# Splitting a layer's first weight tiles earlier: in the down gemm, and between the norm's column blocks

## The reference, cut to what matters

```python
for l in range(DEPTH):                       # DEPTH = 2
    mod = c_act @ w_ada[l] + b_ada[l]
    sh1, sc1, gt1, sh2, sc2, gt2 = split(mod, 6)
    h = rms_norm(x, norm_mix[l]) * (1.0 + sc1) + sh1
    proj = h @ w_in[l]                       # dn_qkv, dn_z, dn_a, dn_b, sw_q, sw_k, sw_v, gate_a, gate_b
    ...
    x = x + gt1 * (merged @ w_o[l])
    h = rms_norm(x, norm_ffn[l]) * (1.0 + sc2) + sh2
    up_act, up_lin = split(h @ w_up[l], 2)
    up_act = causal_dwconv(up_act, ffn_conv[l]) + ffn_conv_b[l]
    x = x + gt2 * ((silu(up_act) * up_lin) @ w_down[l])
# second block, one layer
h = rms_norm_2(x, norm_gain[0])
proj = h @ w_in[0]
...
```

## Time and profile before

| what | value |
|---|---|
| median of 3 runs | 2764.27 us (2758.3 to 2764.56) |
| the profiled execution | 2765.13 us, its span 2763.1 us |
| mean granted TensorE clock | 0.971 |
| PE busy | 2565.5 us, 93% |
| DVE busy | 1444.8 us, 52% |
| ACT busy | 1075.4 us, 39% |
| POOL busy | 918.6 us, 33% |

### The profile page before, as it was taken

The page is one execution under the profiler, slowest core; times in us unless marked ns, Lnnn a source line. Parts: engine busy times, 40 slices in busy tenths (PEclk is TensorE's granted clock), DMA queues, the critical chain, the costliest instruction groups (busy, mean ns, idle before and its releaser), DMA issues. The chain is left out here.

```text
span 2763.1 us, 32968 instructions
## 1 busy us (share of the span) xinstructions
PE 2565.5 (93%) x12929; PEld 2070.7 (75%) x12929; DVE 1444.8 (52%) x2609; ACT 1075.4 (39%) x1872; POOL 918.6 (33%) x402
## 2 busy tenths in 40 slices
PE   5989899899989999989988989999999997899998
PEld 3767768797867888757676878877788886786787
DVE  5289748654535541136993766454344206726323
ACT  3345464245332232243554523543333223236532
POOL 0532231112434444334222211134344443332343
PEclk8999999999999999999999989999999999999999
DMA  6211325643234432222132465422223324731232
GB/s 236 76 62 62 123 69 145 186 133 135 96 103 137 137 102 91 93 92 76 47 123 68 116 165 179 146 87 92 76 92 107 93 98 125 152 101 47 77 121 77
DMA packets 339836, 299.93 MB, mean 109 GB/s; under 512 B 56974, under 2 KB 319460, under 8 KB 338660
## 3 DMA queue, kind: packets, MB, share of 16 engines
q1 hardware_dynamic: 287716, 279.49, 32.5%
q10 hardware_dynamic: 51968, 18.35, 2.7%
HBM read 267.89 MB, written 29.93 MB: 108 GB/s over the span
## 5 line engine op out<-in xcount | busy, mean ns | idle before, releaser
L273 PE MATMUL ps<-hh,split 128*128 128x512 f32 x3808 | 1291.6, 407 | 39.4 <-POOL split L220 24.5
L220 POOL TENSOR_TENSOR split<-ring,split 128x1024 fp32r<-128x1024 f32 (+2 forms) x342 | 814.6, 2383 | 1428.4 <-ACT split L216 1428.4
L273 PEld LDWEIGHTS ps<-hh,split 128*128 128x128 f32 x3808 | 729.0, 191 | 212.5 <-POOL split L220 39.7
L273 PE MATMUL ps<-hl,split 128*128 128x512 f32 x1904 | 753.2, 396 | 0.0
L216 ACT ACTIVATE split<-ring 128x1024 fp32r<-128x1024 f32 (+2 forms) x342 | 347.6, 1018 | 893.1 <-PE ps L273 686.1
L273 PEld LDWEIGHTS ps<-hl,split 128*128 128x128 f32 x1904 | 365.4, 192 | 73.1 <-issue 8.4
L273 PE MATMUL ps<-split 128*128 128x512 f32 x1152 | 285.4, 405 | 9.0 <-DVE split L1095 7.1
L273 PEld LDWEIGHTS ps<-split 128*128 128x128 f32 x1152 | 218.6, 190 | 70.6 <-issue 14.7
L2169 PE MATMUL ps<-split 128*128 128x512 f32 x1056 | 240.2, 389 | 0.0
L2169 PEld LDWEIGHTS ps<-split 128*128 128x128 f32 x1056 | 198.1, 188 | 41.0
L560 POOL TENSOR_TENSOR split<-ring,split 128x1024 fp32r<-128x1024 f32 x32 | 76.1, 2378 | 338.2 <-ACT split L552 338.2
(11 more groups left out here) (408 smaller groups left out, 3178.2 us busy)
## 6 DMA issues: line engine op xcount, KB each, us to landing
ring<-in_w_in_dram SPq DMA_DIRECT2D x60, 1024.0 KB, 5.3
ring<-in_w_up_dram SPq DMA_DIRECT2D x44, 1024.0 KB, 5.1
ring<-in_w_ada_dram SPq DMA_DIRECT2D x64, 512.0 KB, 3.7
ring<-in_w_in_dram SPq DMA_DIRECT2D x34, 512.0 KB, 5.2
big<-in_w_ada_dram SPq DMA_DIRECT2D x16, 1024.0 KB, 8.5
ring<-in_w_down_dram SPq DMA_DIRECT2D x16, 896.0 KB, 4.6
ring<-in_w_swa_out_dram SPq DMA_DIRECT2D x8, 1024.0 KB, 5.0
ring<-in_w_dn_out_dram SPq DMA_DIRECT2D x8, 1024.0 KB, 5.0
```

Of the source, the lines that this page charges most:

```text
L220: on.tensor_tensor(halves(pt, nk)[1], slot(n, nk)[:, :, e * P:(e + 1) * P], halves(pt, nk)[0], ALU.subtract).then_inc(low_made, 1)
L273: ins = nc.tensor.matmul(ps[bank[gt]][0:m, :], w[:, k, :], r[:, k, :], start=(k == 0 and w is w_high and r is rhs[0]), stop=(k == nk - 1 a ...
```

## The change

Five edits. (1) TM's high and low parts get a home of their own (`tm_split`, in `wk` 4, 5, 10, 11) and are made before the layer's block: for layer 0 in the setup block, for layer 1 at the end of layer 0's down gemm. (2) In the layer's block ACT starts with the 16 columns, and puts SW's two high parts behind column blocks 3 and 5 of the norm. (3) The 16 columns' low part goes from POOL to DVE, and POOL starts SW's low parts when seven of the eight `hl` blocks are done. (4) The low parts of the activations follow one block behind instead of two, at all three norms. (5) `mix_sum` moves from `wk` 10 to `kd_flat` in layer 0, since `wk` 10 now holds TM's low part.

```diff
+            tm_split = [split[:, SPLIT_WK + a:SPLIT_WK + a + 2, :].rearrange("p a c -> p (a c)").rearrange(
+                "p (k c) -> p k c", k=KD) for a in (4, 10)]
+            tm_high, tm_low = sem("tm_high"), sem("tm_low")
...
+            def split_tm_high(act, l):
+                act.wait_ge(early[l][TM], 16)
+                nc.scalar.activation(tm_split[0], slot(TM)[:, :, 0:P], ACT.Copy).then_inc(tm_high, 1)
+            def split_tm_low(pool):
+                pool.wait_ge(tm_high, 1)
+                nc.gpsimd.tensor_tensor(tm_split[1], slot(TM)[:, :, 0:P], tm_split[0], ALU.subtract).then_inc(tm_low, 1)
...  (setup block)
+                        split_tm_high(act, 0)
                         mix_rs_of(act)
+                    @block.gpsimd
+                    def _(pool):
+                        split_tm_low(pool)
...  (a layer's first block, ACT)
-                        make_high(act, TM, 0, G_TM)
+                        nc.scalar.sem_inc(high_made, 1)
                         act.wait_ge(ab_in[l], 16)
                         nc.scalar.activation(ab_split[0], ab_raw, ACT.Copy).then_inc(high_made, 1)
                         for k in range(KD):
...
+                            if k in (3, 5):
+                                first_high(act, k // 4)
...
-                        make_high(act, SW, 0, G_SW)
-                        make_high(act, SW, 1, G_SW + 1)
...  (DVE)
-                        for k in range(KD + 2):
+                        for k in range(KD + 1):
...
-                            if k >= 2:
-                                dve.wait_ge(mix_high, k - 1)
+                            if k == 0:
+                                dve.wait_ge(high_made, 2)
+                                nc.vector.tensor_tensor(ab_split[1], ab_raw, ab_split[0], ALU.subtract).then_inc(low_made, 1)
+                            else:
+                                dve.wait_ge(mix_high, k)
...  (POOL)
-                        make_low(pool, nc.gpsimd, TM, 0, G_TM)
-                        pool.wait_ge(high_made, G_TM + 2)
-                        nc.gpsimd.tensor_tensor(ab_split[1], ab_raw, ab_split[0], ALU.subtract).then_inc(low_made, 1)
+                        nc.gpsimd.sem_inc(low_made, 1)
+                        pool.wait_ge(mix_low, KD - 1)
...  (down gemm)
-                    mix_sum = wk[:, 10, :]
+                    mix_sum = kd_flat[:, 0:T] if l + 1 < DEPTH else wk[:, 10, :]
...
+                            if l + 1 < DEPTH and t == 11 and i == 1:
+                                split_tm_high(act, l + 1)
...
+                        if l + 1 < DEPTH:
+                            split_tm_low(pool)
```

More of the change, by code:

```diff
@@ L772, in _ @@
                             pe.wait_ge(mix_low, k + 1)
-                            for e, (w_high, w_low) in enumerate((halves(G_TM, KD), ab_split)):
+                            for e, (w_high, w_low) in enumerate((tm_split, ab_split)):
                                 for w, r in ((w_high, hh), (w_high, hl), (w_low, hh)):
@@ L816, in _, with first_high @@
                     def _(act):
-                        make_high(act, TM, 0, G_TM)
+                        def first_high(act, e):
+                            if e == 0:
+                                act.wait_ge(early[l][SW], 16)
+                            nc.scalar.activation(halves(G_SW + e, KD)[0], slot(SW)[:, :, e * P:(e + 1) * P], ACT.Copy
+                                                 ).then_inc(high_made, 1)
+                        nc.scalar.sem_inc(high_made, 1)
                         act.wait_ge(ab_in[l], 16)
@@ L872, in _ @@
                                                                in1=mix_root, op0=ALU.mult, op1=ALU.mult).then_inc(mix_scaled, 1)
[L873 to L876 removed]
+                            if k == 0:
[3 more added lines that the diff above has]
+                                dve.wait_ge(mix_high, k)
+                                nc.vector.scalar_tensor_tensor(out=hl[:, k - 1, :], in0=big[:, k - 1, :],
+                                                               scalar=mod[:, k - 1:k], in1=hh[:, k - 1, :],
                                                                op0=ALU.add, op1=ALU.subtract).then_inc(mix_low, 1)
@@ L1985, in _ @@
                                                                in1=wk[:, 11, :], op0=ALU.mult, op1=ALU.mult).then_inc(ffn_scaled, 1)
-                            if k >= 2:
-                                dve.wait_ge(ffn_high, k - 1)
-                                nc.vector.scalar_tensor_tensor(out=hl[:, k - 2, :], in0=sq[:, k - 2, :],
-                                                               scalar=mod[:, 22 + k:23 + k], in1=hh[:, k - 2, :],
+                            if k >= 1:
+                                dve.wait_ge(ffn_high, k)
+                                nc.vector.scalar_tensor_tensor(out=hl[:, k - 1, :], in0=sq[:, k - 1, :],
+                                                               scalar=mod[:, 23 + k:24 + k], in1=hh[:, k - 1, :],
                                                                op0=ALU.add, op1=ALU.subtract).then_inc(ffn_low, 1)
@@ L2818, in _ @@
                                                            in1=mix_root, op0=ALU.mult, op1=ALU.mult).then_inc(n_scaled, 1)
-                        if k >= 2:
-                            dve.wait_ge(n_high, k - 1)
-                            nc.vector.tensor_tensor(hl[:, k - 2, :], scaled[:, k - 2, :], hh[:, k - 2, :], ALU.subtract
+                        if k >= 1:
+                            dve.wait_ge(n_high, k)
+                            nc.vector.tensor_tensor(hl[:, k - 1, :], scaled[:, k - 1, :], hh[:, k - 1, :], ALU.subtract
                                                     ).then_inc(n_low, 1)
```

## The result

The changed kernel takes 2744.39 us (median of 6 runs, 2743.51 to 2752.18), the kernel before 2761.93 beside it (median of 6, 2753.4 to 2765.7). The ratio is 0.9947, 95% interval 0.9933 to 0.9962: faster, by 0.5%. The forecast was 2750 (2743 to 2758).

A forecast was written before the change was run, and what follows sets the result against it. PE, busy 93% of the span, was taken as the bound. Gains of 5.3 + 6.7 + 3.4 - 2.0 + 0.9 + 0.5 = 14.8 us took the profiled 2765.13 to 2750.3, the median to 2749.5; forecast 2750, range 2743 to 2758.

The forecast's parts named there:

- The first matmul of a layer: Layer starts: PE's first matmul 2.5 us after the block's start instead of 5.17; 2.65 us gained per layer, 5.3 together.
- the unmeasured term: Layer start: the 16 columns' low part on DVE, found in no profile row, taken as 0.3 us.
- The gap: Between first gemm and SW's first part: PE's 3.36 us idle closes in both layers, 6.7 us gained.
- the two terms that hang on it: Behind the first gemm: closing PE's idle time, 6.7 us, and full clock in SW's first part, 3.4 us.
- The clock's term: SW's first part, both layers: full clock instead of 0.77 once no idle precedes it; 3.4 us gained, from below 0.
- The setup block: Before layer 0: POOL's TM subtraction stops one of DVE's last seven additions; layer 0 starts 2.0 us later.
- The down gemm: Layer 1's TM split, made at layer 0's down gemm end: hidden by 0.3 us; otherwise up to 2 us lost.
- The lag: Low parts one block behind: 0.43 us gained per up gemm, 0.9 for both, and 0.5 us in the second block.
- The terms without the clock: Whole kernel: gains at layer starts 5.3, gap 6.7, up gemms 0.9, second block 0.5, less setup 2.0 us.
- the clock gives more: Rival: six us at half speed from 811.4 and its fellow in layer 1 vanish; 2744 us, chance 0.08.
- the clock gives less: Rival: dips stay or slow phases lengthen, second block's full-speed start may get a dip; 2753.7 to 2757 us, chance 0.19.
- the rule that I read from the earlier trace: DVE beside POOL: an instruction with two SBUF inputs stands still until POOL's is through; one with a PSUM input doesn't.

The follow-up runs named there:

- e_gap: Changed kernel with SW's two high parts put back behind the first gemm's evacuation: 2755.62 us, ratio to the kernel before 0.9981.
- e_setup: Changed kernel with POOL's setup-block subtraction waiting until the block's 32 products and additions are done: 2749.62 us, ratio 0.9951; run again, 2744.58 us, 0.9941.
- e_twice: Changed kernel with POOL's TM subtraction done twice in the setup block, into the same place: 2748.81 us, ratio to the kernel before 0.9954.
- e_lag2: Changed kernel with the low parts two blocks behind again at all three norms: 2747.67 us, ratio to the kernel before 0.9947.
- e_after: The changed kernel once more, with no edit, as yardstick for the variants: 2743.74 us, ratio to the kernel before 0.9935.
- e_lag1_only: The kernel before with only the lag of one block at the three norms: 2757.24 us, ratio to the kernel before 0.9985.

## Why the prediction was right, and where it wasn't

*The first matmul of a layer.* Forecast 2.5 us after the start and 2.65 us won; measured 2.44 and 2.73. Right to 0.1 us, the unmeasured term too: 0.28 us for the 16 columns on DVE, 0.3 taken.

*The gap.* Right: closed in both layers, and nothing waited for the held eighth `hl`. e_gap restores it with one edit and loses 10.3 us in the mean (standard error 1.5); the two terms that hang on it, 6.7 and 3.4, make 10.1. The clock's term is right by itself: SW's first part ran at 1.00 instead of 0.77 in both layers, and again at 0.77 in e_gap.

*The setup block.* Forecast minus 2.0, measured minus 2.3, of which some 0.3 is the later arrival of the weights. e_setup takes the loss away and e_twice adds 1.6 to it, so the cause is shown: POOL's subtraction stands in DVE's way there. The place was wrong: ACT made TM's high part already ahead of 36.3, not at 38.2, and the third group of additions was held, not the last. That place follows the clock: from 28 to 36 us it was 0.79 in the trace of before and 1.00 in that of after, and the squares, which wait for PE there, ended at 37.17 and 35.31. The price was the same, as the chain from the additions to the barrier has no slack in either group.

*The down gemm.* Hidden, as forecast. The high part stands behind the seventh square, and the subtraction was through 0.5 us before the sum of squares.

*The lag.* 0.45 us per up gemm (forecast 0.43) and 0.64 in the second block (0.5); e_lag2 gives them back.

*The sum.* The terms without the clock made 11.4 us, and idle time with the longer setup fell by 11.6. The clock was to give 3.4: in the profiled pair it gave 10.0. About 3.4 of this is the forecast term itself, SW's two first parts. The rest, 6.6, was not in the sum, and it is not shown to be the changed code's own: 2.5 of it lie in each layer's up and down gemms, 1.3 in the six-us window of the dip that the rival "the clock gives more" named (0.72 instead of 0.50), while the second block lost its full-speed start, which the rival "the clock gives less" named. In layer 1 0.9 us went back in the first gemm itself: its clock was 0.79 instead of 0.86. The steps fall elsewhere in each program and execution: e_after, the same program, had 1.00 again in the second block. In the profiles of the kernels with the gap (before, e_gap, e_lag1_only) PE was busy 2561.4 to 2566.1 us, in those without it (the other seven) 2552.0 to 2564.0; the means, 2564.3 and 2558.0, lie 6 us apart, but the two overlap. Over all runs the difference is 15.2 us with 14.8 forecast, and 15.2 - 11.6 leaves the clock 3.6. The standard error of the 15.2 is about 1.2 us, and the 11.6 stems from one pair of profiles.

The record has a second measure, the span and the granted clock of each single execution. Span times (1 - clock) is an estimate of what the lower clock cost it; it is a little too large, since it also counts the lower clock while PE idled. Its mean is 73.8 us for the kernel before (34 executions that have a clock on record), 73.4 for e_gap (12) and 70.6 for the changed kernel (11). So the clock gave 3.3 and 2.9 us, each with a standard error of about 1.5: in size the forecast's 3.4, and about two standard errors from nothing. What remains of the span fell by 11.8 us, where the code's terms made 11.4.

*The time itself.* 2744.4 came out 5.6 us below 2750. None of the code's terms explains it: the base did. The three runs shown had a median of 2764.27 and the profiled one 2765.13, while 40 runs of that kernel have a mean of 2760.5. Its runs reach from 2748.3 to 2767.9. From 2760.5 the same sum gives 2745.7. So the gain was forecast well, and the range held because it was wide enough for a base that was some 4 us too high: 2744.4 lies 1.4 us above its lower end.

*The parts together.* 10.3 (gap, e_gap) + 2.8 (lag, e_lag2) leaves 2.1 of the 15.2 for TM's early split with the 16 columns on DVE. The forecast's terms for it give the same, and to this closeness by luck, as the 2.1 has a standard error of 2.2: twice 2.65, less the 0.6 that the lag brings alone at each start (e_lag1_only), less 2.0 in the setup block. By these terms half of what the early split wins is lost there.

## What to carry to other kernels

Find, for each idle stretch of the bounding engine, the one transform that released it, and ask which earlier idle stretch of its engine could hold it: two moved conversions were worth two thirds of this gain, at no work saved. Before work goes to an "idle" POOL, look at what DVE does beside it; here a subtraction on POOL cost a DVE instruction on SBUF up to its own length (2.0 us of 2.34 in the setup block), and a wait that moved POOL by 7 us took the cost away. When an edit is worth less than the spread of single executions, split the span into busy and idle time of the bounding engine by stage, with the same number of matmuls on both sides: idle repeated within 2 us where totals spread over 10 to 20.

## What the runs showed of the hardware

POOL's 128 x 1024 subtraction (2.34 to 2.50 us) held one DVE instruction at a time: additions and `hl` with two SBUF inputs took 2.3 to 2.9 us instead of 0.75 where most of it was left. The instruction that was held needn't have two tensors as inputs: the tensor-scalar of e_twice went from 0.48 to 2.10 us. That falls outside the rule that I read from the earlier trace rows, and the trace of before had it already. From there, a subtraction of two SBUF tensors in the same up gemm as line 2035, and a tensor-scalar of one (duration ns min/median/max):

```profile
L2047 DVE TENSOR_TENSOR split<-wk,split x44: 682/1618/2559, 826.1 to 2177.9; 128x512 fp32r<-128x512 f32 x44
L464 DVE TENSOR_SCALAR vs<-ring,c_act x32: 336/346/2532, 416.9 to 1758.4; 128x256 f32<-128x256 f32 x32
```

In that trace 22 of the 44 instructions at line 2047 started with about 2.0 us of a POOL subtraction left, and each took 2.55 to 2.56 us. Of the 88 at line 2035, 48 started with 0.5 to 2.0 us of one left, and none took more than 0.751 us. So it isn't a short overlap that spares line 2035; that it is the PSUM input fits, and no run here puts that one input elsewhere.

Executions of one and the same program spread over 10 us (e_setup, 11 runs) and 11 us (the changed kernel, 11 runs) to 20 us (before, 40 runs), with the same instructions. In the profiles, programs with the same code in a stretch differ there in PE's busy time alone: 688.6 and 693.6 us for 3672 matmuls. Behind gaps of about 3 us stood stretches at half clock of 0 to 6 us, and they changed where the gap stayed the same: 1.00 and 0.77 behind the two gaps of e_lag1_only, and 0.51 and 1.00 over 6 us behind the same 2.96 us gap of the second block in the changed kernel's two profiles. What sets where the step falls stays open. The Trainium skill ("TensorE: Matmul & The Clock Gate", section "What's actually happening") says that the monitor runs freely; these rows fit that, and no run here shows more.

Left open: the same early split at the up gemm, where PE idles 2.96 us in each layer and once more in the second block, wasn't tried. Nor was the early split with the 16 columns left on POOL.
